# A ring of three for the modulation weights of the decode stage, and output weights ahead of the router's

## Chip, core and metric

One NeuronCore of a Trainium2 chip runs the whole step as one program. The metric is the device time of one execution in microseconds (us); the lower the better. PE is TensorE (PEld its weight loads), DVE VectorE, ACT ScalarE, POOL GpSimd, SP SyncE, which mostly issues DMAs.

## What is computed

One layer of a decoder step for a prompt of 2048 tokens and 8 decode tokens, in float32. What matters here is the decode side and the modulation:

```python
mod = (jax.nn.silu(c) @ w_ada + b_ada)[:, None, :]
sh1, sc1, gt1, sh2, sc2, gt2 = jnp.split(mod, 6, axis=-1)
...
s = jnp.einsum('bthe,btkhe->bthk', q, kg)     # decode: 8 tokens, three windows of 129 keys each
p = jnp.exp(s - m[..., None])
num = jnp.einsum('bthk,btkhe->bthe', p, vg)
...
conv = jax.nn.silu(layernorm(causal_dwconv(cext, conv_w, conv_b), ln_g, ln_b))
x = x + gt1 * (jnp.concatenate([att, conv], axis=-1) @ w_out)
h2 = rmsnorm(x, g_n2) * (1 + sc2) + sh2
x = x + gt2 * hierarchical_moe(h2, ...)
```

`w_ada` is 1024 x 6144 for 9 rows of `c` (8 decode rows and the prompt's). The first third, `sh1` and `sc1`, is made in the first stage; the other two thirds (gates and the second norm's vectors) are made in the decode stage.

## The kernel before

Stages follow one another, each in a block of its own with a barrier at its end: projection of all rows, attention of the prompt, the decode stage (`decode_mixers`), output projection and routing (`output_projection_and_routing`), experts, last norm. In a block every engine runs its own list of instructions in the order written, and semaphores tie them together.

**Decode stage** (L1187 to L1430). Keys, values and queries of the decode tokens (`dec_k`, `dec_v`, `dec_q`) were loaded during the attention stage.

- Modulation (L1384 to L1396): 16.8 MB of `w_ada` stream through `WAD`, a ring of two halves. A chunk is 512 of the 4096 columns; a half of it (512 of the 1024 rows, 1 MB, one DMA at L1253) is used by 16 matmuls `MPD<-WAD,CT` (four row blocks by four column quarters; the trace shows each as two, so x32 for a half); after both halves four matmuls add the bias `BAD` (L1395), ACT copies the sum from PSUM to `MOD_` (L1282), and after chunk 7 it is stored as `mod_rows` (L1298). SP issues a half when PE has used the one that was in its buffer (`w_used`).
- Scores (L1271, L1303 to L1327): for each of 8 batch entries b the product `dec_k` * `dec_q` (128x1536) and a sum over 64. POOL makes the products of odd b in `TMPP`, DVE those of even b in `TMP`, and DVE all the sums. Between them DVE makes the newest token's score: product QK, sum `S0D`, product `S0X` (two inputs in SBUF), which PE's first matmul (L1399) waits for.
- Convolution: DVE multiplies `ST` by the taps `CWR` (L1327), PE sums over the taps (L1408, `CP<-ST`).
- PE's order: N0 (L1399), chunks 0 to 3, transposed scores (L1404, `STP`), taps (L1408), transposed probabilities (L1412, `PTP`), L1415, chunks 4 and 5, values (L1422, `OD<-dec_v`), gathering (L1426), chunks 6 and 7.

**Output stage** (from L1433): for 17 tiles of rows a round mixes the three attention branches (`NB`, `STAT`) and the convolution's columns (`CC`), multiplies by `WO` (4 MB), normalises, and routes with `WR`. SP loads ahead of the rounds: 11 vectors (`GATE`, `GAIN`, `SHIFT` from `mod_rows`, `G2`, `LNG`, `LNB`, `BR`; L1507 to L1514), the first tile (L1519 to L1521), `WR`, `WO`, `lower`. DVE and POOL begin when all 11 vectors are in (`mods_in`); the load of the second tile waits until the first is mixed; PE's `project` (L1837) of the first tile stands behind `turn_conv` (L1818) of the second.

Of the kernel before, what the change touches and what calls it, by code (L numbers as in the profile page):

```python
# [13 lines left out]
AX = mybir.AxisListType  # L14
# [3 lines left out]
P = 128  # L18
SEQ = 2048
DEC = 8  # L20
D = 1024
KD = D // P
# [1164 lines left out]
def decode_mixers(nc, t, dr, const, const_at, state):  # L1187
# [7 lines left out]
    with ExitStack() as ctx:  # L1195
# [22 lines left out]
        WA, BA, MO = sb("WAD", [P, 2, KD // 2, 512]), sb("BAD", [1, 2, 512]), sb("MOD_", [P, NCH, P])  # L1218
        ada_in, b_in = ([sem(f"{x}{p}") for p in range(2)] for x in ("dec_ada_in", "dec_ada_b_in"))
# [16 lines left out]
        with nc.Block() as block:  # L1236
            @block.sync
            def _(sp):
                sp.dma_start(R[:], dr["dec"].rearrange("n b c -> b n c")).then_inc(rows_in, 16)
# [7 lines left out]
                w = t["w_ada"][0].rearrange("(k p) n -> p k n", p=P)  # L1247
# [12 lines left out]
                sp.dma_start(dr["mix"], MIX[:]).then_inc(mix_out, 16)  # L1260
                sp.wait_ge(mix_out, 16)
                sp.wait_ge(state_out, 32)

            @block.gpsimd
            def _(pool):
                pool.wait_ge(dq_in, 16)
                pool.wait_ge(dk_in, 48)
                for n, b in enumerate(range(1, DEC, 2)):
                    if n:
                        pool.wait_ge(odd_red, n)  # L1270
                    pool.tensor_tensor(TMPP[:], CK[:, b], QB[:, b, None, :].to_broadcast([P, 3, DATT]), ALU.mult).then_inc(odd_mul, 1)  # L1271
                pool.wait_ge(var_ready, 1)
                pool.tensor_tensor(VE[:], MV[:, 1:2], const("eps", DEC), ALU.add).then_inc(rs_ready, 1)
                pool.wait_ge(rs_ready, 1)
                pool.tensor_tensor(RS[:], VE[:], const("neghalf", DEC), ALU.pow).then_inc(rs_ready, 1)

            @block.scalar
            def _(act):
                def take_modulation(chunks):
                    for n in chunks:  # L1280
                        act.wait_ge(mod_in_psum, n + 1)
                        nc.scalar.copy(MO[:, n], MP[n % 2][:]).then_inc(mod_ready, 1)  # L1282

# [4 lines left out]
                nc.scalar.activation(PE_[:], SS[:], ACT.Exp, bias=NMD[:], scale=1.0, accum_out=LD[:]).then_inc(exp_ready, 1)  # L1288
                act.wait_ge(p8_psum, 1)
                nc.scalar.copy(P8[:], P8P).then_inc(p8_ready, 1)  # L1290
                take_modulation(range(4, 6))
                act.wait_ge(cstep, 7)
                nc.scalar.activation(TH[:], CVN[:], ACT.Tanh, scale=0.5).then_inc(th_ready, 1)
                take_modulation(range(6, NCH))
                act.wait_ge(mod_ready, NCH)
                for q in range(4):
                    out = dr["mod"][:, MOD_FIRST * 512:].rearrange("r (n q c) -> q r n c", q=4, c=P)
                    act.dma_start(out[q], MO[q * 32:q * 32 + DEC + 1]).then_inc(mod_out, 16)  # L1298
                act.wait_ge(mod_out, 64)

            @block.vector
            def _(dve):
# [6 lines left out]
                for n in range(DEC // 2):  # L1309
                    if n:  # L1310
                        dve.wait_ge(even_red, n)
                    nc.vector.tensor_tensor(TMP[:], CK[:, 2 * n], QB[:, 2 * n, None, :].to_broadcast([P, 3, DATT]), ALU.mult).then_inc(even_mul, 1)
                    dve.wait_ge(even_mul, n + 1)
                    reduced(2 * n, TMP, even_red)
                    if n == 0:
                        dve.wait_ge(rows_in, 16)
                        nc.vector.tensor_tensor(QK0[:], R[:, 0], R[:, 1], ALU.mult).then_inc(new_step, 1)
                        dve.wait_ge(new_step, 1)
                        nc.vector.tensor_reduce(S0[:], QK0[:].rearrange("b (h e) -> b h e", e=DH), AX.X, ALU.add).then_inc(new_step, 1)
                        dve.wait_ge(new_step, 2)  # L1320
                        nc.vector.tensor_tensor(S0X[:], const("samebatch", DEC).rearrange("b (a h) -> b a h", h=HEADS), S0[:, None, :].to_broadcast([DEC, DEC, HEADS]),
                                                ALU.mult).then_inc(new_spread, 1)
                    dve.wait_ge(odd_mul, n + 1)
                    reduced(2 * n + 1, TMPP, odd_red)
# [56 lines left out]
            def _(pe):  # L1381
                def modulation(chunks):
                    for n in chunks:
                        if n > 1:  # L1384
                            pe.wait_ge(mod_ready, n - 1)
                        for half in range(2):
                            pe.wait_ge(ada_in[half], n * 16 + 16)
                            for k in range(KD // 2):
                                for q in range(4):
                                    mm = nc.tensor.matmul(MP[n % 2][q * 32:q * 32 + 32], CT[:, half * KD // 2 + k], WA[:, half, k, q * P:q * P + P],  # L1390
# [9 lines left out]
                modulation(range(4))  # L1400
                pe.wait_ge(even_red, DEC // 2)
                pe.wait_ge(odd_red, DEC // 2)
                for n in range(3):
                    mm = nc.tensor.transpose(STP[:, n], SC[:, n], const("ident"))  # L1404
                mm.then_inc(s_turned, 1)
# [3 lines left out]
                mm.then_inc(conv_sum, 1)  # L1409
                pe.wait_ge(p_ready, 1)  # L1410
# [5 lines left out]
                modulation(range(4, 6))  # L1416
# [14 lines left out]
def output_projection_and_routing(nc, t, dr, const, const_at, state):  # L1431
# [27 lines left out]
    with ExitStack() as ctx:  # L1459
# [44 lines left out]
        with nc.Block() as block:  # L1504
            @block.sync
            def _(sp):
                for n, (dst, part) in enumerate(((GATE, 2), (GAIN, 4), (SHIFT, 3))):  # L1507
                    sp.dma_start(dst[:, 0], dr["mod"][DEC:DEC + 1, part * D:(part + 1) * D].to_broadcast([P, D])).then_inc(mods_in, 16)
                    sp.dma_start(dst[0:DEC, 1], dr["mod"][0:DEC, part * D:(part + 1) * D]).then_inc(mods_in, 16)
                sp.dma_start(G2[:], t["g_norm2"].to_broadcast([P, D])).then_inc(mods_in, 16)  # L1510
                sp.dma_start(LNG[:], t["ln_g"].to_broadcast([P, DCONV])).then_inc(mods_in, 16)
                sp.dma_start(LNB[:], t["ln_b"].to_broadcast([P, DCONV])).then_inc(mods_in, 16)
                sp.dma_start(BR[:, 0:GROUPS], t["b_router_group"].to_broadcast([P, GROUPS])).then_inc(mods_in, 16)
                sp.dma_start(BR[:, GROUPS:], t["b_router_expert"].to_broadcast([P, NEXP])).then_inc(mods_in, 16)  # L1514

# [106 lines left out]
            def _(act):  # L1622
# [21 lines left out]
                def route_exps(i):  # L1644
# [3 lines left out]
                    nc.scalar.activation(EV[:], DV[:], ACT.Exp).then_inc(gap_exp, 1)  # L1648

# [709 lines left out]
```

## Time and profile before

| what | value |
|---|---|
| median of 3 runs | 2475.18 us (2471.99 to 2478.70) |
| profiled execution, its own time | 2476.43 us |
| its span, first to last instruction | 2474.9 us |
| mean granted TensorE clock | 0.926 |
| decode stage, first DMA to first DMA of the next stage | 957.98 to 1037.33 us |
| of it PE busy, DVE busy, ACT busy, POOL busy (958 to 1037) | 41.73, 36.97, 3.66, 18.82 us |
| same stretch: DMA engines' busy share, rate | 0.71, 237 GB/s |
| output stage, first DMA to the first projection | 1037.33 to 1071.64 us |

The span is the sum of the stages, since barriers part them; so a stage is read by what its own last instruction waited for, not by the busy shares of the whole. A row of the timeline gives start, duration, engine, line, operation, what is written and read, and in brackets how long the engine had been idle and what ended that.

### The profile page before, as it was taken

Reading aid. Unit: us, or ns where it says so; the run is one execution under the profiler, and the core shown is the slowest. Engines: PE = TensorE matmul, PEld = TensorE weight load, DVE = VectorE, ACT = ScalarE, POOL = GpSimd, SP = SyncE. Lnnn points to the kernel's source line nnn. Section 1 sums busy time; section 2 is a strip of 40 time slices with the busy share of each in tenths; the row PEclk is TensorE's granted clock in tenths of the full one; section 3 lists DMA queues with packets and bytes.
Section 4 is the critical chain, followed back from the end, with each engine's and each line's share of the span. In section 5 each row is a group of like instructions: output and inputs, shape, how many; then the busy total and the mean of one; then the engine's idle time right before and its main releaser. Section 6 shows DMA issues by size and latency. Waiting matters only on the chain. (4 is left out here: it accounts for less than half of the span.)

```text
span 2474.9 us, 36684 instructions
## 1 busy us (share of the span) xinstructions
PE 2129.0 (86%) x11790; PEld 1630.7 (66%) x11791; DVE 1646.7 (67%) x3121; ACT 1099.2 (44%) x1979; POOL 642.1 (26%) x519
## 2 busy tenths in 40 slices
PE   5999999996999984459999939999999999999920
PEld 3788888885777773225555537888888888888810
DVE  2568888885666676147888656846563846656868
ACT  2311111114777781002222226856554757567833
POOL 1024444420111113035666521000000000000056
PEclk8999999998999996679999959999999999999965
DMA  8855555565664454668433156977765859658977
GB/s 267 276 193 187 187 187 203 192 207 193 203 235 135 140 181 163 227 257 312 131 130 128 70 196 246 398 263 263 262 234 190 315 214 353 251 208 300 397 271 297
DMA packets 220147, 560.78 MB, mean 227 GB/s; under 512 B 26685, under 2 KB 40341, under 8 KB 218904
## 3 DMA queue, kind: packets, MB, share of 16 engines
q1 hardware_dynamic: 179708, 439.45, 50.4%
q0 software_dynamic: 26016, 79.49, 8.9%
q10 hardware_dynamic: 14340, 40.78, 4.4%
q8 instruction: 46, 0.75, 0.1%
q14 instruction: 37, 0.30, 0.0%
HBM read 461.18 MB, written 171.04 MB: 255 GB/s over the span
## 5 line engine op out<-in xcount | busy, mean ns | idle before, releaser
L591 DVE SCALAR_TENSOR_TENSOR ARENA<-ARENA,TAPW 128x512 f32<-128x512 f32 (+3 forms) x493 | 293.3, 673 | 0.0
L1837 PE MATMUL OP<-WO,MT 128*128 128x512 f32 x544 | 258.3, 636 | 0.0
L417 POOL TENSOR_TENSOR MS<-SSQ,K 128x1 f32<-128x1 f32 x17 | 168.3, 9901 | 293.8 <-ACT H L460 293.8
L2103 DVE TENSOR_TENSOR GE<-SE,BE 128x256 f32<-128x256 f32 x98 | 36.8, 417 | 272.4 <-PE BE L2145 270.1
L1837 PEld LDWEIGHTS OP<-WO,MT 128*128 128x128 f32 x544 | 111.1, 208 | 135.7 <-issue 135.7
L710 PE MATMUL PJ<-WIN_H,HTH 128*128 128x512 f32 x680 | 174.0, 399 | 15.2 <-ACT HTH L466 11.7
L1017 ACT ACTIVATE PR<-SBX,NM 128x256 f32<-128x256 f32 (+1 forms) x384 | 171.9, 456 | 1.4 <-DVE NM L955 1.4
L2001 POOL DMA_INDIRECT XG<-h_rows,IDX x50 | 52.3, 1046 | 453.6 <-PE XP L2134 437.5
L714 PE MATMUL PJ<-WIN_H,HTL 128*128 128x512 f32 x680 | 168.4, 390 | 0.0
L718 PE MATMUL PJ<-WIN_L,HTH 128*128 128x512 f32 x680 | 168.0, 389 | 0.0
L492 ACT ACTIVATE ARENA<-PJ 128x512 f32<-128x512 f32 x51 | 30.4, 598 | 289.4 <-PE PJ L718 289.4
L710 PEld LDWEIGHTS PJ<-WIN_H,HTH 128*128 128x128 f32 x680 | 128.2, 191 | 46.6 <-ACT HTH L466 15.9
L2092 DVE TENSOR_TENSOR LO<-W1E,HI 128x2048 fp32r<-128x2048 f32 x64 | 143.6, 2283 | 3.9 <-ACT HI L2046 3.9
L714 PEld LDWEIGHTS PJ<-WIN_H,HTL 128*128 128x128 f32 x680 | 128.2, 189 | 27.0
L718 PEld LDWEIGHTS PJ<-WIN_L,HTH 128*128 128x128 f32 x680 | 127.6, 188 | 26.5
L2092 DVE TENSOR_TENSOR LO<-W3E,HI 128x2048 fp32r<-128x2048 f32 x64 | 143.6, 2284 | 0.6 <-ACT HI L2046 0.6
L2092 DVE TENSOR_TENSOR LO<-W2E,HI 128x2048 fp32r<-128x2048 f32 x64 | 143.6, 2284 | 0.0
L2046 ACT CAST HI<-W1E 128x2048 fp32r<-128x2048 f32 x64 | 120.1, 1902 | 31.1 <-DMA W1E<-in_w_expert_gate 30.6
L952 DVE CUSTOM_DVE_ANT_0 SBX<-S,BIAS 128x256 f32<-128x256 f32 (+1 forms) x384 | 117.4, 362 | 22.7 <-issue 22.7
L2046 ACT CAST HI<-W2E 128x2048 fp32r<-128x2048 f32 x64 | 120.6, 1912 | 25.2 <-ACT YE L2066 14.4
L2046 ACT CAST HI<-W3E 128x2048 fp32r<-128x2048 f32 x64 | 120.0, 1917 | 1.6 <-DMA W3E<-in_w_expert_up 1.5
L2013 POOL DMA_DIRECT2D IDX<-slot_tokens x48 | 27.4, 571 | 358.0 <-issue 247.2
(297 smaller groups left out, 4584.8 us busy)
## 6 DMA issues: line engine op xcount, KB each, us to landing
W1E<-in_w_expert_gate SPq DMA_DIRECT2D x64, 1024.0 KB
W3E<-in_w_expert_up SPq DMA_DIRECT2D x64, 1024.0 KB
W2E<-in_w_expert_down SPq DMA_DIRECT2D x64, 1024.0 KB, 11.3
expert_rows<-YE ACTq DMA_DIRECT2D x49, 512.0 KB, 5.7
expert_rows<-NOROWS POOLq DMA_DIRECT2D x3, 5632.0 KB, 20.8
WAD<-in_w_ada SPq DMA_DIRECT2D x16, 1024.0 KB, 5.4
X<-in_x_prompt SPq DMA_DIRECT2D x31, 512.0 KB
QN<-q_rows SPq DMA_DIRECT2D x48, 256.0 KB, 3.0
```

The lines of the kernel that those rows point to most:

```text
L417: pool.tensor_tensor(MS[:], SSQ[:], const("eps"), ALU.add).then_inc(ms_ready, 1)
L591: ins = nc.vector.scalar_tensor_tensor(out=out, in0=src, scalar=tap, in1=out, op0=ALU.mult, op1=ALU.add)
L710: nc.tensor.matmul(PJ[:, n], HTH[:, k], WH[:, n, k], start=k == 0, stop=False)
L714: nc.tensor.matmul(PJ[:, n], HTL[:, k], WH[:, n, k], start=False, stop=False)
L718: mm = nc.tensor.matmul(PJ[:, n], HTH[:, k], WL[:, n, k], start=False, stop=k == KD - 1)
L952: nc.vector.tensor_tensor_reduce(SBX[hh][:, h, 0:wide], SP_[hh][:, at_bank(h), 0:wide], bias, 1.0, -3e38, ALU.add, ALU.max, ml[:, head:hea ...
L1017: ins = nc.scalar.activation(PR[hh][:, h, 0:w], SBX[hh][:, h, 0:w], ACT.Exp, bias=NM[:, head:head + 1], scale=1.0, accum_out=ML[g.q][:, HE ...
L1837: mm = nc.tensor.matmul(OP[:, n * 512:(n + 1) * 512], MT[:, k], WO[:, k, n * 512:(n + 1) * 512], start=k == 0, stop=k == KD - 1)
L2001: pool.indirect_dma_start(XG[:], None, dr["h2"], bass.IndirectOffsetOnAxis(ap=IDX[:].bitcast(U32), axis=0)).then_inc(x_in, 16)
L2046: nc.scalar.copy(HI[n][:, cols], raw[n][:, cols]).then_inc(hi_ready[n], 1)
L2092: nc.vector.tensor_tensor(LO[n][:, cols], raw[n][:, cols], HI[n][:, cols], ALU.subtract).then_inc(lo_ready[n], 1)
L2103: nc.vector.tensor_tensor(G[:, cols], S[:, cols], BP[:, cols], ALU.mult).then_inc(g_ready, 1)
```

## The change

In the decode stage: the ring of `w_ada` has three buffers, each with its own semaphore, and half x is issued when half x-3 has been used; SP issues `DROWS`, then three halves, two biases, and only then the loads for the convolution, `OWN` last; the other six biases are issued by ACT behind its copies. POOL makes the products of b = 1, 3, 5, DVE the other five. DVE's order is written anew. PE's order: N0, chunks 0 and 1, taps, chunks 2 and 3, transposed scores, chunk 4, transposed probabilities, L1415's product, chunk 5, values, gathering, chunks 6 and 7. In the output stage the 11 vectors are issued by ACT instead of SP, and SP issues `WO` ahead of `WR`.

```diff
-        WA, BA, MO = sb("WAD", [P, 2, KD // 2, 512]), sb("BAD", [1, 2, 512]), sb("MOD_", [P, NCH, P])
-        ada_in, b_in = ([sem(f"{x}{p}") for p in range(2)] for x in ("dec_ada_in", "dec_ada_b_in"))
+        RINGS = 3
+        WA, BA, MO = sb("WAD", [P, RINGS, KD // 2, 512]), sb("BAD", [1, 2, 512]), sb("MOD_", [P, NCH, P])
+        ada_in, b_in = [sem(f"dec_ada_in{p}") for p in range(RINGS)], [sem(f"dec_ada_b_in{p}") for p in range(2)]
+        BY_POOL = (1, 3, 5)
...
             def _(sp):
+                def weights(x):
+                    n, half = divmod(x, 2)
+                    col = (MOD_FIRST + n) * 512
+                    if x >= RINGS:
+                        sp.wait_ge(w_used, x + 1 - RINGS)
+                    sp.dma_start(WA[:, x % RINGS], w[:, half * KD // 2:(half + 1) * KD // 2, col:col + 512]).then_inc(ada_in[x % RINGS], 16)
+
                 sp.dma_start(R[:], dr["dec"].rearrange("n b c -> b n c")).then_inc(rows_in, 16)
-                at, width = const_at["ownhead"]
-                sp.dma_start(OWN[:], t["constants"][:, at:at + width]).then_inc(own_in, 16)
+                for x in range(RINGS):
+                    weights(x)
+                for n in range(2):
+                    sp.dma_start(BA[:, n], t["b_ada"][0:1, (MOD_FIRST + n) * 512:(MOD_FIRST + n + 1) * 512]).then_inc(b_in[n], 16)
...
-                for n in range(NCH):
-                    col = (MOD_FIRST + n) * 512
-                    for half in range(2):
-                        if n:
-                            sp.wait_ge(w_used, n * 2 + half - 1)
-                        sp.dma_start(WA[:, half], w[:, half * KD // 2:(half + 1) * KD // 2, col:col + 512]).then_inc(ada_in[half], 16)
-                    if n > 1:
-                        sp.wait_ge(mod_in_psum, n - 1)
-                    sp.dma_start(BA[:, n % 2], t["b_ada"][0:1, col:col + 512]).then_inc(b_in[n % 2], 16)
+                at, width = const_at["ownhead"]
+                sp.dma_start(OWN[:], t["constants"][:, at:at + width]).then_inc(own_in, 16)
+                for x in range(RINGS, 2 * NCH):
+                    weights(x)
...
-                for n, b in enumerate(range(1, DEC, 2)):
+                for n, b in enumerate(BY_POOL):
...
                         nc.scalar.copy(MO[:, n], MP[n % 2][:]).then_inc(mod_ready, 1)
+                        if n + 2 < NCH:
+                            col = (MOD_FIRST + n + 2) * 512
+                            act.dma_start(BA[:, n % 2], t["b_ada"][0:1, col:col + 512]).then_inc(b_in[n % 2], 16)
...
+                own_scores(0)
+                dve.wait_ge(rows_in, 16)
+                nc.vector.tensor_tensor(QK0[:], R[:, 0], R[:, 1], ALU.mult).then_inc(new_step, 1)
+                pool_scores(0)
+                dve.wait_ge(new_step, 1)
...
+                own_scores(1)
                 dve.wait_ge(conv_in, 16 * 9)
                 nc.vector.tensor_tensor(ST[:], ST[:], CWR[:, None, :].to_broadcast([4 * TS, 2, DCONV]), ALU.mult).then_inc(taps_ready, 1)
+                pool_scores(1)
+                own_scores(2)
+                own_scores(3)
+                pool_scores(2)
+                own_scores(4)
...
             def _(sp):
-                for n, (dst, part) in enumerate(((GATE, 2), (GAIN, 4), (SHIFT, 3))):
-                    sp.dma_start(dst[:, 0], dr["mod"][DEC:DEC + 1, part * D:(part + 1) * D].to_broadcast([P, D])).then_inc(mods_in, 16)
...
                 load(0, 0)
+                sp.dma_start(WO[:], t["w_out"][0].rearrange("(k p) n -> p k n", p=P)).then_inc(weights_in, 16)
                 sp.dma_start(WR[:, :, 0:GROUPS], t["w_router_group"][0].rearrange("(k p) n -> p k n", p=P)).then_inc(weights_in, 16)
                 sp.dma_start(WR[:, :, GROUPS:], t["w_router_expert"][0].rearrange("(k p) n -> p k n", p=P)).then_inc(weights_in, 16)
-                sp.dma_start(WO[:], t["w_out"][0].rearrange("(k p) n -> p k n", p=P)).then_inc(weights_in, 16)
...
+                for n, (dst, part) in enumerate(((GATE, 2), (GAIN, 4), (SHIFT, 3))):
+                    act.dma_start(dst[:, 0], dr["mod"][DEC:DEC + 1, part * D:(part + 1) * D].to_broadcast([P, D])).then_inc(mods_in, 16)
```

TensorE in the decode stage, before, from chunk 3 to chunk 4 (a row `MPD<-WAD,CT` x32 is a whole chunk here, `MPD<-BAD,K` its bias):

```order
L1390 MATMUL MPD<-WAD,CT 32x128 x32
L1395 MATMUL MPD<-BAD,K 32x128 x4
L1404 MATMUL STP<-K,SC 64x128 x3
L1408 MATMUL CP<-ST,K 8x512 x2
L1412 MATMUL PTP<-K,SS 128x64 x3
L1415 MATMUL SMALLD<-P0X,K 8x8
L1390 MATMUL MPD<-WAD,CT 32x128 x32
```

and now, from the taps to chunk 5:

```order
L1427 MATMUL CP<-ST,K 8x512 x2
L1414 MATMUL MPD<-WAD,CT 32x128 x32
L1419 MATMUL MPD<-BAD,K 32x128 x4
L1414 MATMUL MPD<-WAD,CT 32x128 x32
L1419 MATMUL MPD<-BAD,K 32x128 x4
L1433 MATMUL STP<-K,SC 64x128 x3
L1414 MATMUL MPD<-WAD,CT 32x128 x32
L1419 MATMUL MPD<-BAD,K 32x128 x4
L1438 MATMUL PTP<-K,SS 128x64 x3
L1441 MATMUL SMALLD<-P0X,K 8x8
L1414 MATMUL MPD<-WAD,CT 32x128 x32
```

The taps' two matmuls (`CP<-ST`) moved ahead of chunks 2 and 3, and chunk 4 now stands between the transposed scores (`STP`) and the transposed probabilities (`PTP`).

VectorE at the start of the decode stage, before (the first product to the second POOL sum):

```order
L1312 TENSOR_TENSOR TMP<-dec_k,dec_q 128x1536
L1307 TENSOR_REDUCE SC<-TMP 128x3x8
L1317 TENSOR_TENSOR QK<-DROWS 8x512
L1319 TENSOR_REDUCE S0D<-QK 8x8
L1321 TENSOR_TENSOR S0X<-K,S0D 8x64
L1307 TENSOR_REDUCE SC<-TMPP 128x3x8
L1312 TENSOR_TENSOR TMP<-dec_k,dec_q 128x1536
```

and now:

```order
L1326 TENSOR_TENSOR TMP<-dec_k,dec_q 128x1536
L1319 TENSOR_REDUCE SC<-TMP 128x3x8
L1336 TENSOR_TENSOR QK<-DROWS 8x512
L1319 TENSOR_REDUCE SC<-TMPP 128x3x8
L1339 TENSOR_REDUCE S0D<-QK 8x8
L1341 TENSOR_TENSOR S0X<-K,S0D 8x64
L1326 TENSOR_TENSOR TMP<-dec_k,dec_q 128x1536
L1319 TENSOR_REDUCE SC<-TMP 128x3x8
L1345 TENSOR_TENSOR ST<-ST,CWR 120x1024
L1319 TENSOR_REDUCE SC<-TMPP 128x3x8
```

The sum of POOL's first product (`SC<-TMPP`) now stands ahead of `S0D` and `S0X`, and the taps' product (`ST<-ST,CWR`) in front of its second sum.

## Rows read from the trace of the kernel before

**Rows 1.** Stretch of the decode stage: us, busy PE, PEld, DVE, ACT, POOL; PEclk, DMA share, GB/s

```profile
969.90:997.40 27.50, 16.91 (x288) 11.61 (x288) 15.00 (x10) 0.80 (x3) 12.94 (x3) 0.56 0.86 290
```

**Rows 2.** Waits, 957.9 to 1031.6 us: total, times, longest

```profile
ACT MOD_ L1282 <- PE MPD L1395: 57.5, 8, 9.0
PE MPD L1390 <- DMA WAD<-in_w_ada: 23.2, 12, 4.2
```

**Rows 3.** Issue to landing, DMAs of L1253 (WAD), then of L1519 (NB)

```profile
DMA to landing us min/median/max: 5.0/5.4/8.7
...
DMA to landing us min/median/max: 4.3/4.6/11.8
```

**Rows 4.** Timeline, the modulation on SP's queue and PE

```profile
978.58 3.59 SPq L1253 DMA_DIRECT2D WAD<-in_w_ada  x2
983.80 1.93 PE L1390 MATMUL MPD<-WAD,CT 128*32 128x128 f32 x32 [1.48 <-DMA WAD<-in_w_ada]
991.09 1.94 PE L1390 MATMUL MPD<-WAD,CT 128*32 128x128 f32 x32 [0.94 <-DMA WAD<-in_w_ada]
1008.48 1.94 PE L1390 MATMUL MPD<-WAD,CT 128*32 128x128 f32 x32 [4.00 <-DMA WAD<-in_w_ada]
1011.17 1.42 PE L1390 MATMUL MPD<-WAD,CT 128*32 128x128 f32 x32 [0.75 <-DMA WAD<-in_w_ada]
1030.82 0.65 PE L1395 MATMUL MPD<-BAD,K 1*32 1x128 f32 x8
```

**Rows 5.** Timeline, products and scores on DVE and POOL

```profile
958.08 3.41 POOL L1271 TENSOR_TENSOR TMPP<-dec_k,dec_q 128x1536 f32<-128x1536 f32 x1 [10.90 <-POOLq L191]
958.10 5.00 DVE L1312 TENSOR_TENSOR TMP<-dec_k,dec_q 128x1536 f32<-128x1536 f32 x1 [13.60 <-PEq L191]
...
966.22 0.21 DVE L1321 TENSOR_TENSOR S0X<-K,S0D 8x64 f32<-8x64 f32 x1
...
968.02 1.74 DVE L1312 TENSOR_TENSOR TMP<-dec_k,dec_q 128x1536 f32<-128x1536 f32 x1
968.17 4.90 POOL L1271 TENSOR_TENSOR TMPP<-dec_k,dec_q 128x1536 f32<-128x1536 f32 x1 [6.68 <-DVE SC L1307]
...
988.27 1.22 DVE L1327 TENSOR_TENSOR ST<-ST,CWR 120x1024 f32<-120x1024 f32 x1
```

**Rows 6.** Timeline, PE's other work in the decode stage

```profile
997.43 0.85 PE L1404 MATMUL STP<-K,SC 128*64 128x128 f32 x3
998.21 3.58 PE L1408 MATMUL CP<-ST,K 120*8 120x512 f32 x4
1001.72 0.40 PE L1412 MATMUL PTP<-K,SS 64*128 64x64 f32 x3
1012.86 5.36 PE L1422 MATMUL OD<-dec_v,PTD 128*32 128x512 f32 x48
1019.14 0.42 PE L1390 MATMUL MPD<-WAD,CT 128*32 128x128 f32 x6
```

**Rows 7.** Timeline, SP's queue: first weights, first load of the next stage

```profile
963.36 0.95 SPq L1253 DMA_DIRECT2D WAD<-in_w_ada  x2
...
1037.33 0.36 SPq L1508 DMA_DIRECT2D GATE<-mod_rows  x1
```

**Rows 8.** Timeline, start of the output stage

```profile
1046.96 5.17 SPq L1550 DMA_DIRECT2D WR<-in_w_router_expert  x1
1050.76 2.35 DVE L1673 SCALAR_TENSOR_TENSOR GAIN<-GAIN,G 128x1024 f32<-128x1024 f32 x2 [29.92 <-DMA BR<-in_b_router_expert]
1052.18 0.95 SPq L1551 DMA_DIRECT2D WO<-in_w_out  x1
...
1064.03 0.49 SPq L1521 DMA_DIRECT2D CC<-conv_cols  x1
...
1070.73 1.12 PE L1818 MATMUL CP<-K,CC 128*128 128x128 f32 x4 [5.10 <-DMA CC<-conv_cols]
```

**Rows 9.** Stretch of the output stage, columns as in Rows 1

```profile
1048.00:1053.00 5.00, 0.00 (x0) 0.00 (x0) 2.24 (x2) 0.00 (x0) 0.00 (x0) 0.50 0.77 213
```

More of the change, by code:

```diff
@@ L1238, in _ @@
             def _(sp):
+                w = t["w_ada"][0].rearrange("(k p) n -> p k n", p=P)
+                def weights(x):
[4 more added lines that the diff above has]
+                    sp.dma_start(WA[:, x % RINGS], w[:, half * KD // 2:(half + 1) * KD // 2, col:col + 512]).then_inc(ada_in[x % RINGS], 16)
                 sp.dma_start(R[:], dr["dec"].rearrange("n b c -> b n c")).then_inc(rows_in, 16)
-                at, width = const_at["ownhead"]
-                sp.dma_start(OWN[:], t["constants"][:, at:at + width]).then_inc(own_in, 16)
+                for x in range(RINGS):
+                    weights(x)
+                for n in range(2):
+                    sp.dma_start(BA[:, n], t["b_ada"][0:1, (MOD_FIRST + n) * 512:(MOD_FIRST + n + 1) * 512]).then_inc(b_in[n], 16)
                 for b in range(4):
@@ L1288, in _ @@
                 nc.scalar.activation(PE_[:], SS[:], ACT.Exp, bias=NMD[:], scale=1.0, accum_out=LD[:]).then_inc(exp_ready, 1)
+                take_modulation(range(4, 5))
                 act.wait_ge(p8_psum, 1)
                 nc.scalar.copy(P8[:], P8P).then_inc(p8_ready, 1)
-                take_modulation(range(4, 6))
+                take_modulation(range(5, 6))
                 act.wait_ge(cstep, 7)
@@ L1307, in reduced, with own_scores @@
                     nc.vector.tensor_reduce(SC[:, :, b * HEADS:(b + 1) * HEADS], tmp[:].rearrange("p n (h e) -> p n h e", e=DH), AX.X, ALU.add).then_inc(done, 1)
-                for n in range(DEC // 2):
+                own = [b for b in range(DEC) if b not in BY_POOL]
+                def own_scores(n):
                     if n:
                         dve.wait_ge(even_red, n)
-                    nc.vector.tensor_tensor(TMP[:], CK[:, 2 * n], QB[:, 2 * n, None, :].to_broadcast([P, 3, DATT]), ALU.mult).then_inc(even_mul, 1)
+                    nc.vector.tensor_tensor(TMP[:], CK[:, own[n]], QB[:, own[n], None, :].to_broadcast([P, 3, DATT]), ALU.mult).then_inc(even_mul, 1)
@@ L1313, in _ @@
                     dve.wait_ge(even_mul, n + 1)
[L1314 to L1322, printed above, removed]
@@ L1323, in _, with pool_scores @@
-                    dve.wait_ge(odd_mul, n + 1)
-                    reduced(2 * n + 1, TMPP, odd_red)
+                    reduced(own[n], TMP, even_red)
+                def pool_scores(n):
+                    dve.wait_ge(odd_mul, n + 1)
+                    reduced(BY_POOL[n], TMPP, odd_red)
+                own_scores(0)
+                dve.wait_ge(rows_in, 16)
+                nc.vector.tensor_tensor(QK0[:], R[:, 0], R[:, 1], ALU.mult).then_inc(new_step, 1)
+                pool_scores(0)
@@ L1326, in _ @@
+                dve.wait_ge(new_step, 1)
+                nc.vector.tensor_reduce(S0[:], QK0[:].rearrange("b (h e) -> b h e", e=DH), AX.X, ALU.add).then_inc(new_step, 1)
+                dve.wait_ge(new_step, 2)
+                nc.vector.tensor_tensor(S0X[:], const("samebatch", DEC).rearrange("b (a h) -> b a h", h=HEADS), S0[:, None, :].to_broadcast([DEC, DEC, HEADS]),
+                                        ALU.mult).then_inc(new_spread, 1)
+                own_scores(1)
                 dve.wait_ge(conv_in, 16 * 9)
@@ L1386, in modulation @@
                         for half in range(2):
-                            pe.wait_ge(ada_in[half], n * 16 + 16)
+                            x = 2 * n + half
+                            pe.wait_ge(ada_in[x % RINGS], x // RINGS * 16 + 16)
                             for k in range(KD // 2):
                                 for q in range(4):
-                                    mm = nc.tensor.matmul(MP[n % 2][q * 32:q * 32 + 32], CT[:, half * KD // 2 + k], WA[:, half, k, q * P:q * P + P],
+                                    mm = nc.tensor.matmul(MP[n % 2][q * 32:q * 32 + 32], CT[:, half * KD // 2 + k], WA[:, x % RINGS, k, q * P:q * P + P],
                                                           start=half == 0 and k == 0, stop=False)
@@ L1399, in _ @@
                 nc.tensor.matmul(N0P, S0X[:].rearrange("b a h -> b (a h)"), const("ones", DEC)[:, 0:1], start=True, stop=True).then_inc(new_psum, 1)
[L1400 to L1405, printed above, removed]
+                modulation(range(2))
                 pe.wait_ge(taps_ready, 1)
@@ L1409, in _ @@
                 mm.then_inc(conv_sum, 1)
+                modulation(range(2, 4))
+                pe.wait_ge(even_red, DEC - len(BY_POOL))
+                pe.wait_ge(odd_red, len(BY_POOL))
+                for n in range(3):
+                    mm = nc.tensor.transpose(STP[:, n], SC[:, n], const("ident"))
+                mm.then_inc(s_turned, 1)
+                modulation(range(4, 5))
                 pe.wait_ge(p_ready, 1)
@@ L1415, in _ @@
                 nc.tensor.matmul(P8P, const("ofbatch", BH), P0X[:], start=True, stop=True).then_inc(p8_psum, 1)
-                modulation(range(4, 6))
+                modulation(range(5, 6))
                 pe.wait_ge(ptd_ready, 1)
@@ L1506, in _ @@
             def _(sp):
-                for n, (dst, part) in enumerate(((GATE, 2), (GAIN, 4), (SHIFT, 3))):
-                    sp.dma_start(dst[:, 0], dr["mod"][DEC:DEC + 1, part * D:(part + 1) * D].to_broadcast([P, D])).then_inc(mods_in, 16)
[L1509 to L1514, printed above, removed]
                 def load(i, row):
@@ L1648, in route_exps @@
                     nc.scalar.activation(EV[:], DV[:], ACT.Exp).then_inc(gap_exp, 1)
+                for n, (dst, part) in enumerate(((GATE, 2), (GAIN, 4), (SHIFT, 3))):
+                    act.dma_start(dst[:, 0], dr["mod"][DEC:DEC + 1, part * D:(part + 1) * D].to_broadcast([P, D])).then_inc(mods_in, 16)
+                    act.dma_start(dst[0:DEC, 1], dr["mod"][0:DEC, part * D:(part + 1) * D]).then_inc(mods_in, 16)
+                act.dma_start(G2[:], t["g_norm2"].to_broadcast([P, D])).then_inc(mods_in, 16)
+                act.dma_start(LNG[:], t["ln_g"].to_broadcast([P, DCONV])).then_inc(mods_in, 16)
+                act.dma_start(LNB[:], t["ln_b"].to_broadcast([P, DCONV])).then_inc(mods_in, 16)
+                act.dma_start(BR[:, 0:GROUPS], t["b_router_group"].to_broadcast([P, GROUPS])).then_inc(mods_in, 16)
+                act.dma_start(BR[:, GROUPS:], t["b_router_expert"].to_broadcast([P, NEXP])).then_inc(mods_in, 16)
                 act.sem_inc(x2_out, 16)
```

1 line of the change is left out of this document (removed).

## The prediction

> **What bounds the kernel now.** The stages are separated by barriers, so what a stage saves comes off the span. I read first the busy time of the engines in stretches, then the waits of the decode stage, then its timeline, then the same for the start of the output stage. From 969.9 to 997.4 us PE was busy 16.91 of 27.5 us, its granted clock mostly the lower of the two, while the DMA engines were 0.86 busy at 290 GB/s [rows 1]. PE's own waits name the cause: 23.2 us for the weights WAD; ACT waited 57.5 us for the finished sums, so it has room [rows 2]. The stage is a queue of 16 halves of 1 MB (8 chunks of two), numbered 0 to 15 here. A half takes 5.4 us (median) from issue to landing [rows 3], 5.2 where nothing is ahead of it (half 4, issued at 978.58, used from 983.80); PE uses it in 1.93 us [rows 4].
>
> With two buffers a buffer comes round in 5.2 + 1.93, about 7.2 us: half 4 starts at 983.80, half 6 at 991.09, 7.29 apart, so 3.6 us for each half [rows 4]. Yet two halves that are both in the queue land 2.69 us apart (1008.48 and 1011.17) [rows 4]. So the depth of the ring, not the transfer, sets the pace. Besides, the ring stands still when TensorE turns to other work: half 12 lands late behind one such pause, halves 14 and 15 behind another.
>
> **The ring of three.** Three halves per 7.2 us would be 2.4 us each; the transfer needs 2.6 to 2.7. I take 2.6, a bound by transfer. The first half is issued at about 958.4, where it was 963.36 (DROWS goes ahead of it at 958.0) [rows 7]; halves 0, 1, 2 land near 963.6, 966.2, 968.8. This early start is mostly lost, though, since PE's first matmul waits for S0X:
>
> **DVE and POOL.** Where POOL's product of 128x1536 started first (958.08, 3.41 us), DVE's took 5.00 us and ended 1.6 us after it; where DVE's started first (968.02, 1.74 us), POOL's took 4.90 [rows 5]. The two products with both inputs in SBUF exclude each other. Now DVE adds up POOL's first product before it makes S0 and S0X; so POOL's second product starts at about 967.4, while DVE is in the 0.67 us sum S0, and S0X, a product of two SBUF tiles, waits for its end at 970.8. S0X ends at 971.0 instead of 966.4 [rows 5]. The trace shows no small product behind a POOL product; if S0X is not held, it ends at 968.2, and the whole timetable is 2.7 earlier. I take 971.0, by the nearest row, the held product of 5.00.
>
> Scores: DVE now makes 5 products and 8 sums of 1.75, 1.55 for the new token and 1.22 for the taps (25.5), plus 3.3 held at the start, 2.6 at S0X, 1.6 at its fourth product: from 958.1 to about 991.2, against 988.3 before (the taps started at 988.27) [rows 5]. PE asks for them only after chunk 3, so 3 us later costs nothing while chunk 3 ends after 991.2. The loads for the taps now stand behind 3 MB of weights, 0.8 MB that should be in by 972; DVE asks for them at 974.6.
>
> **Timetable of PE** (landing = the later of issue + 5.2 and the half before + 2.6; a bias 0.65 [rows 4]). Halves 0 to 2 run from 971.4 to 977.8 with the bias of chunk 0. Half 3, issued at 973.4, lands at 978.6; chunk 1 ends at 981.2. Then the taps' matmuls, moved here: 3.6 us [rows 6], to 984.8; they are not hidden, since half 4 is there at 981.2. Halves 4, 5, 6 follow to 991.2; half 7 (issued 986.8) lands at 992.0; chunk 3 ends at 994.6. Transposing the scores takes 0.85 [rows 6]. Chunk 4 (halves 8, 9, both there) fills 995.4 to 999.9; DVE's softmax meanwhile needs 3.4 from the end of the transposes (998.3 to 1001.7 before [rows 6]), done at 998.8, so this wait of PE goes. Turning the probabilities takes 0.6. Chunk 5 (half 11, issued 997.4, lands at 1002.6) ends at 1005.1. The values and their gathering take 6.3 (1012.86 to 1019.14 [rows 6]): 1011.4. Halves 12 to 14 were fetched meanwhile. Half 15 can be issued only when 12 is used, at 1013.4, and lands at 1018.6; chunk 7 ends at 1021.1. Before, it ended at 1031.5 (1030.82 + 0.65 [rows 4]). **Term 1: -10.4 us.** The way from there to the next stage (its first load at 1037.33 [rows 7]) is unchanged: 5.9. The two copies of the convolution state and the store of MIXD follow half 15 on SP, at about 1014 to 1016, covered by halves 14 and 15 and those 5.9 us.
>
> Six biases of 2 KB move to ACT, 0.4 us each behind a copy: ACT has 57.5 us of waits, and each bias has two chunks of time. Nothing. If a bias landed late, PE would wait with two halves in hand. OWN goes last and is asked for at 1010: nothing.
>
> **The output stage.** ACT now issues the 11 loads of vectors (2.73 MB, 5.7 us of issuing, while it has nothing to do), SP starts with the branch rows at once and issues the 4 MB WO before WR. Before, WR's second issue held SP from 1046.96 for 5.17 us, WO was issued at 1052.18, and from 1048 to 1053 the DMA engines moved only 213 GB/s [rows 8, 9]; that hole is now filled. DVE starts with GAIN when all 11 are in, at 1050.76 [rows 8]. They now share the engines with the rows and WO. If they are held back only by their own gaps, they land as before; if the queues share evenly, 5.5 MB must move at some 400 GB/s (1.05 MB in 2.6 us), 13.7 us, with 2.6 around it (what a half's 5.2 has beyond its transfer): 1053.6, +2.9. I take +1.5, the middle, since both ends rest on one stretch each. On the other side, the second tile's columns were issued at 1064.03 behind WO and landed at 1070.7, 6.7 us, and PE's first projection follows at once [rows 8]. With WO gone from the queue I take 4.7 (the rows NB before them land in 4.6 as a median [rows 3]): -2.0. **Term 2: -0.5 us**, bounds -3.3 and +2.9.
>
> A page speaks against this term. By the Trainium skill, "DMA: Bandwidth & Descriptors" (queues, rings and completion order), each DMA engine takes packets in turn from the queues that have work, and issuing from more engines saves issue time only. By this rule alone the vectors come 2.9 later and term 2 is +0.9; the low 213 GB/s of [rows 9] says that there was idle time to fill, which the rule leaves open.
>
> **Sum:** -10.9. The profiled execution (span 2474.9, its own time 2476.43) would become 2465.5; it lay 1.25 above the median of 2475.18, so the predicted median is 2464.3. About 0.3%, 7.4 us, can be told from no change.
>
> **Rivals.**
> A. S0X is not held: 2.7 better, term 1 is -13.1: 2461.6. For it: no row shows a small product held. Against: the product of 5.00. Chance 0.10.
> B. Transfer rate: with three in flight a half still needs 3.6 us, as from 969.9 to 997.4. Then half 11 lands at 978.6 + 8 x 3.6 = 1007.4, half 15 at 1021.8, end 1024.3: term 1 is -7.2, 2467.5. For it: the DMA share of 0.86 [rows 1]. Against: halves 2.69 apart [rows 4]. Chance 0.15.
> C. The loads for the taps come late behind the weights, and DVE, waiting in order, holds all later scores. It decides from 978 on (3.4 us of slack before chunk 3's end); at 981 the scores come at 997.6, 3 us late: 2467.3. Chance 0.10.
> D. Slower: the vectors of the output stage starve behind WO, WR and the rows and land when all is in, at about 1066 (WO then took to 1052.18 + 13), 15.3 us later than 1050.76, and POOL and DVE wait for them. With term 1 that is +4.9: 2480. It makes the kernel slower once the delay is over 10.4, and by more than 0.3% from 17.8. For it: one queue of 4 KB rows against many small ones. Against: the vectors are issued at the same time as the rows. Chance 0.07.
> My forecast has 0.58, its own bounds from 2460 to 2468.
>
> **Chances.** Faster by over 0.3% (below 2467.8): 0.9 of the forecast, all of A, a third of B, half of C: 0.72. Slower by over 0.3%: half of D, 0.03. Within: 0.25. The range 2460.0 to 2472.0 holds the forecast, A, B and C and leaves out D and mishaps of more than 8 us.
>
> **What would show it.** Right: halves of WAD about 2.6 us apart in PE's timeline; S0X ending near 971; its first weights waiting for PE, not PE for them; the score transposes right behind chunk 3 at 994 to 995; PE's wait before turning the probabilities gone; the output stage's first load near 1027; GAIN 13.5 to 16.5 after it (13.4 before); PE's first projection 34 after it. Wrong: a wait of DVE for the loads of the taps, or of PE for a bias; halves 3.6 apart; GAIN more than 17 us after the start; SP held by WR's issue beyond the moment the second tile's rows are wanted.

## The result, and the profile after

The change makes the kernel faster: 2462.79 us (median of 12 runs, 2458.63 to 2470.12) against 2476.94 us before (12 runs), ratio 0.9947 with the 95% interval 0.9936 to 0.9958, so 14.1 us; repeated later, 0.9944 (0.9930 to 0.9957). The forecast was 10.9 us.

| stage, from its first DMA to the next stage's | before | after | difference |
|---|---|---|---|
| the two stages ahead of the decode stage | 957.98 | 955.79 | -2.19 |
| decode | 79.35 | 67.38 | -11.97 |
| output projection and routing | 412.08 | 411.96 | -0.12 |
| experts | 919.54 | 920.08 | +0.54 |
| last norm | 105.95 | 105.19 | -0.76 |
| span | 2474.9 | 2460.4 | -14.5 |

The change touches only the second and third of these. The first row shows how far one execution of the same code can differ from another: over the 14 profiles of this case the decode stage starts 952.29 to 958.92 us after the start of the span, though none of them changes what comes ahead of it. The decode stage in stretches (columns as in [rows 1]), then its waits:

```profile
969.90:997.40 27.50, 19.72 (x358) 12.83 (x350) 21.77 (x21) 2.04 (x7) 4.88 (x1) 0.75 0.99 337
```

```profile
ACT MOD_ L1290 <- PE MPD L1419: 43.4, 8, 8.3
...
PE MPD L1414 <- DMA WAD<-in_w_ada: 11.1, 8, 3.0
```

Against [rows 1] the DMA engines went from 0.86 to 0.99 busy and from 290 to 337 GB/s; PE's waits for weights fell from 23.2 to 11.1 us. The timeline of DVE, POOL and PE in the decode stage after the change:

```profile
965.03 3.42 POOL L1279 TENSOR_TENSOR TMPP<-dec_k,dec_q 128x1536 f32<-128x1536 f32 x1 [5.73 <-DVE SC L1319]
965.58 2.94 DVE L1341 TENSOR_TENSOR S0X<-K,S0D 8x64 f32<-8x64 f32 x1
...
972.36 1.22 DVE L1345 TENSOR_TENSOR ST<-ST,CWR 120x1024 f32<-120x1024 f32 x1 [0.38 <-DMA LBD<-in_ln_b]
...
977.62 1.88 PE L1427 MATMUL CP<-ST,K 120*8 120x512 f32 x4
...
986.45 1.94 PE L1414 MATMUL MPD<-WAD,CT 128*32 128x128 f32 x32 [0.67 <-DMA WAD<-in_w_ada]
986.96 1.75 DVE L1319 TENSOR_REDUCE SC<-TMP 128x24 f32<-128x1536 f32 x1
...
989.05 1.94 PE L1414 MATMUL MPD<-WAD,CT 128*32 128x128 f32 x32 [0.66 <-DMA WAD<-in_w_ada]
...
991.26 0.52 PE L1433 MATMUL STP<-K,SC 128*64 128x128 f32 x3
...
1001.85 5.36 PE L1448 MATMUL OD<-dec_v,PTD 128*32 128x512 f32 x48
...
1015.18 1.94 PE L1414 MATMUL MPD<-WAD,CT 128*32 128x128 f32 x32 [3.02 <-DMA WAD<-in_w_ada]
1017.05 0.65 PE L1419 MATMUL MPD<-BAD,K 1*32 1x128 f32 x8
```

Halves 6 and 7 come 2.60 us apart, where halves came 3.6 apart ([rows 4]: 983.80 and 991.09 for two of them). That is the best pair, though: half 4 was used at 980.18, so halves 4 to 7 come 2.96 us apart on average. S0X, 0.21 us in [rows 5], lasted 2.94: POOL's product had started 0.55 us before S0X did, and S0X ended 0.07 us after the product. DVE's last sum of scores ends at 988.71, and PE turns to the scores (`STP`) only at 991.26. The last half is waited for, as forecast, but for 3.02 us, where the timetable has 0.7 (half 14 used up at 1017.9, half 15 there at 1018.6): PE was through half 14 in 1.08 us instead of 1.93, at the higher clock. The start of the output stage:

```profile
1023.17 0.37 SPq L1536 DMA_DIRECT2D NB<-branch_rows  x1
...
1025.43 7.81 SPq L1567 DMA_DIRECT2D WR<-in_w_router_group  x1
...
1033.28 11.32 SPq L1568 DMA_DIRECT2D WR<-in_w_router_expert  x1
...
1041.65 2.35 DVE L1699 SCALAR_TENSOR_TENSOR GAIN<-GAIN,G 128x1024 f32<-128x1024 f32 x2 [31.82 <-DMA BR<-in_b_router_expert]
...
1053.47 0.48 SPq L1538 DMA_DIRECT2D CC<-conv_cols  x1
...
1058.69 1.12 PE L1844 MATMUL CP<-K,CC 128*128 128x128 f32 x4 [3.64 <-DMA CC<-conv_cols]
```

GAIN starts 18.48 us after the stage's first DMA (13.43 in [rows 7, 8]), 5.05 later; the second tile's columns land in 5.22 us instead of 6.7; PE's first projection comes at 36.43 instead of 34.31.

### The profile page after: what moved, and what is told of

Its sections match the earlier page's. It is cut to its first block and busy times, and to the rows that moved or that the text cites. A ratio compares the mean times of both kernels' runs of the same rounds, so it can differ in the third digit from the quotient of the medians.

```text
span 2460.4 us, 36684 instructions
## 1 busy us (share of the span) xinstructions
PE 2119.0 (86%) x11790; PEld 1625.5 (66%) x11791; DVE 1650.2 (67%) x3122; ACT 1098.9 (45%) x1979; POOL 634.2 (26%) x518
## 5 line engine op out<-in xcount | busy, mean ns | idle before, releaser
L710 PE MATMUL PJ<-WIN_H,HTH 128*128 128x512 f32 x680 | 173.9, 398 | 14.5 <-ACT HTH L466 11.7
L710 PEld LDWEIGHTS PJ<-WIN_H,HTH 128*128 128x128 f32 x680 | 128.1, 191 | 45.9 <-ACT HTH L466 15.9
```

The lines of the kernel that those rows point to most:

```text
L710: nc.tensor.matmul(PJ[:, n], HTH[:, k], WH[:, n, k], start=k == 0, stop=False)
```

## Experiments

All are measured against the kernel before; "stage" is the decode stage in the profiled execution, of which each run has one. Of the same code its length varies: 79.35 and 82.49 us for the old one (before, e2), 67.08 to 68.73 us in four of five executions of the new one (after, e1, e3, e11) and 72.40 in the fifth (e4). A difference of a few microseconds between two stages is therefore no proof by itself; where it is used below, the timeline inside the stage is shown for it.

### Which half of the change: e1_decode_only, e2_output_only

```diff
 e1: decode_mixers of the change, output_projection_and_routing of before
 e2: decode_mixers of before, output_projection_and_routing of the change
```

> The change's decode stage alone, output stage as before. Theory: the decode stage is 67.4 us long (first DMA to the next stage's first DMA) as in the full change, 12.0 shorter than the 79.35 of before, and the output stage keeps its 412.1 us with GAIN 13.4 us and the first projection 34.3 us after its start: 12 us faster than before, 0.995. Rival 1 (the output part of the change costs 2 us, as its first projection 2.1 later says): this kernel is 2 us faster than the full change. Rival 2 (the output part gains 2, as forecast with its lower bound): it is 2 us slower than the full change.

> The change's output stage alone, decode stage as before. Theory: decode stage 79.4 us; GAIN 18.5 us and the first projection 36.4 us after the output stage's start (13.4 and 34.3 before), the stage as a whole 411.9 as in the full change, since the next rounds wait for DMAs anyway: same time as before. Rival 1: 2 us slower, stage 414. Rival 2: 2 us faster.

e1: 2460.38 us, ratio 0.9929 (0.9915 to 0.9943); stage 67.08. e2: 2476.14 us, ratio 0.9994 (0.9985 to 1.0003); GAIN at 16.61 and the first projection at 34.18 us. So the whole gain is the decode stage's, and the output part is worth nothing that can be told on its own.

### What makes the output part: e3_wo_first, e4_vectors_act, e11_change_again

```diff
 e3 (on e1's output stage):
-                WR (two loads), WO
+                WO, WR (two loads)          # the 11 vectors stay on SP
 e4 (on the change):
-                WO, WR (two loads)
+                WR (two loads), WO          # the 11 vectors stay on ACT
 e11: the change itself
```

> New decode stage; output stage with WO ahead of WR but the 11 vectors on SP as before. If sharing the DMA engines between two queues made GAIN late (theory), GAIN is back at 13.4 us after the start, WO's early issue fills the hole, the second tile's columns land in about 5.2 instead of 6.7 us, and the first projection comes at about 32.8: 1.5 better than e1_decode_only. Rival (WO itself in front costs as much as it gives, since WR's small packets then run alone later): first projection at 34 or later.

> New decode stage; output stage with the 11 vectors on ACT but WR ahead of WO as before. Theory (WO's 4 MB take half of the engines from the vectors): WR's issue holds WO back by 6 us or more, so GAIN comes at 15 to 16 us after the start, between 13.4 and 18.5. Rival (two queues of small packets, WR and BR, hinder each other): GAIN stays at 18 or later.

> The change itself once more beside the others, for the output stage. Theory (its output part costs 1.5 to 2 us against that of before): GAIN at 16.6 to 18.5 and first projection at 34.2 to 36.4 us after the stage's start again, and the time 1 to 3 us above e1_decode_only's 2460.4. Rival (no cost): the time within 1 us of it. Decode stage 67 to 69 us.

| output stage | GAIN after start, us | first projection after start, us |
|---|---|---|
| as before (before, e1, e6, e7, e8) | 12.24 to 13.43 | 33.43 to 34.31 |
| of the change (after, e2, e5, e11) | 16.61 to 18.48 | 34.18 to 36.43 |
| vectors on SP, WO first (e3, e9, e10) | 11.61 to 13.92 | 32.22 to 34.57 |
| vectors on ACT, WR first (e4, e12) | 14.43, 14.64 | 32.33, 32.40 |

In time e3 is 2462.83 us (ratio 0.9931, 0.9914 to 0.9948) and e4 2459.54 (0.9924, 0.9909 to 0.9940); neither can be told from e1. The vectors are late by 3 to 5 us only where they go on ACT's queue and WO stands ahead of WR on SP's; with WR first, whose issue held SP for 7.84 us in e12, WO starts 10.1 us into the stage and the vectors are 1.0 to 1.2 us late. That supports the sharing of the DMA engines with WO. e3's gain of 1.5 did not come again in e9 and e10. In time, e11 (2462.43) and the change lie 2 us above e1, with overlapping intervals; the mean first projection of the four is 1.6 us later (35.4 against 33.8). So the output part costs one to two microseconds at the first tile. Little of it reaches the end of the stage: from its first load to the experts' first load the stage took 408.66 to 412.08 us in the five profiles with the output part of before (mean 410.6) and 411.03 to 412.09 in the four with that of the change (mean 411.6). The means are 1.0 apart, inside the spread of the same code.

### Ring or order: e5_ring_two, e6_ring_only, e8_old_pe_order

```diff
 e5 (on the change):
-        RINGS = 3
+        RINGS = 2
 e6 (on before; each buffer with a semaphore of its own, and PE's index to match):
-        WA = sb("WAD", [P, 2, KD // 2, 512])
+        WA = sb("WAD", [P, 3, KD // 2, 512])
+                        x = 2 * n + half
+                        if x > 2:
+                            sp.wait_ge(w_used, x - 2)
 e8 (on e1), PE, in short; ACT's copies follow the same order:
-                modulation(range(2)); taps; modulation(range(2, 4)); scores turned; modulation(range(4, 5)); probabilities turned; modulation(range(5, 6))
+                modulation(range(4)); scores turned; taps; probabilities turned; modulation(range(4, 6))
```

> The full change with a ring of two again. Theory (the ring carries most of the gain): a half every 3.6 us again; only the wait before the probabilities and the taps' matmuls are still covered, so the decode stage is 75 to 77 us, about 9 more than the 67.4 of the full change and 3 less than before. Rival (order of work carries it): 71 us or less.

> The kernel before with a ring of three and nothing else. Theory: halves 2.6 to 2.8 us apart up to chunk 3, which ends near 33 us after the stage's start (39.5 before); taps and softmax hold PE as before, the stage is 69 to 71 us. Rival (the early start and the order carry the gain): 75 or more.

> New decode stage but PE's order of before (taps after the scores, probabilities ahead of chunks 4 and 5); output stage as before. Theory: taps (1.9 to 3.6 us) and the softmax (3.4, partly beside the taps) are uncovered again, but the three buffers fill meanwhile and are used faster than they come, so the stage is only 1 to 3 us longer than 67.1. Rival (the order matters more than the ring): 4 us or more.

e5: 2476.69 us, ratio 0.9999 (0.9987 to 1.0011), stage 83.02. The rest of the change without the third buffer gains nothing that can be told; the 3 us expected for it did not appear. PE in e5, weights of chunks 1 and 2:

```profile
977.77 1.94 PE L1414 MATMUL MPD<-WAD,CT 128*32 128x128 f32 x32 [3.64 <-DMA WAD<-in_w_ada]
981.21 1.93 PE L1414 MATMUL MPD<-WAD,CT 128*32 128x128 f32 x32 [1.50 <-DMA WAD<-in_w_ada]
```

Its half 2 is used 20.3 us into the stage (19.2 before). It could be issued only when half 0 had been used, and PE could not begin before S0X, which POOL held until 12.74 us. So SP issued half 2 at 972.52, 15.1 us into the stage, and it was used 5.25 us later; the small loads were through by then, the DMA engines stood at 0.24 busy from 969.43 to 971.43 and idle for the 2 us after. By this timeline the early issue buys two halves only, and the hold of S0X costs what they gain. A ring of two without that hold was not run, so e5 shows that the rest of the change as it stands needs the third buffer, and not that no order of work could gain without it.

e6: 2464.96 us, ratio 0.9952 (0.9934 to 0.9969), stage 71.34: the third buffer alone gives 8.0 of the 12.0 in the stage, and in time it can't be told from the whole change (0.9947). Its chunk 3 ends 34.5 us into the stage, no later than that of the change (35.5; before 39.5), so up to there the third buffer gives all of it. By the end of chunk 5 it is 3.2 us behind the change, and the values, which ran partly at the low clock (6.75 against 5.36 us), add 1.4; what follows gives 0.6 back. In e6, PE's halves 2 and 3 are 2.70 us apart:

```profile
974.92 1.94 PE L1392 MATMUL MPD<-WAD,CT 128*32 128x128 f32 x32 [0.20 <-DMA WAD<-in_w_ada]
977.62 1.93 PE L1392 MATMUL MPD<-WAD,CT 128*32 128x128 f32 x32 [0.77 <-DMA WAD<-in_w_ada]
```

The mean from half 2 to half 7 is 2.89 us in e6, 3.57 in the kernel before.

e8: 2466.18 us, ratio 0.9949 (0.9933 to 0.9965), stage 72.42, 5.3 more than e1; the expected 1 to 3 fell. Its interval overlaps with e1's (0.9915 to 0.9943). Its PE:

```profile
994.29 0.85 PE L1427 MATMUL STP<-K,SC 128*64 128x128 f32 x3
995.06 3.57 PE L1431 MATMUL CP<-ST,K 120*8 120x512 f32 x4
998.57 0.40 PE L1435 MATMUL PTP<-K,SS 64*128 64x64 f32 x3
...
999.02 1.95 PE L1413 MATMUL MPD<-WAD,CT 128*32 128x128 f32 x64
...
1006.78 1.94 PE L1413 MATMUL MPD<-WAD,CT 128*32 128x128 f32 x32 [4.44 <-DMA WAD<-in_w_ada]
```

For the 4.7 us from 994.29 to 999.02 no buffer comes free. The three full ones are then used in a burst, and PE waits 4.44 us for half 11, whose issue had to wait for the first of the burst. (1.4 of the 5.3 are the values, which ran in part at the low clock, 6.78 against 5.36 us.) A pause of PE longer than the ring's stock is a pause of the transfer: that is what the new order removes. Since one stage length proves little, the stretch in question is compared over all profiles: from the end of chunk 3 to the end of chunk 5 PE took 14.75 us in e6 and 14.94 in e8, with three buffers and the old order, and 10.59 to 13.57 in the eight profiles with three buffers and the change's order (after, e1, e3, e4, e7, e9, e11, e12). So the order gives 1.2 to 4.4 us there. With two buffers and the change's order (e5) the stretch took 14.41, against 15.43 and 16.82 with the old.

### PE's start and the scores: e7_s0x_early, e9_taps_on_act, e10_chunk4_first

```diff
 e7 (on e1), DVE:
-                own_scores(0); QK; pool_scores(0); S0; S0X; own_scores(1)
+                own_scores(0); QK; S0; S0X; pool_scores(0); own_scores(1)
 e9 (on e7; WO first): the nine loads for the taps and OWN
-                sp.dma_start(...)
+                act.dma_start(...)          # ahead of ACT's first copy
 e10 (on e9), PE, in short; ACT's copies follow the same order:
-                modulation(range(2, 4)); scores turned; modulation(range(4, 5)); probabilities turned; modulation(range(5, 6))
+                modulation(range(2, 5)); scores turned; modulation(range(5, 6)); probabilities turned
```

> New decode stage with S0X made ahead of the sum of POOL's first product; output stage as before. Theory (S0X was held by POOL's product): S0X takes 0.2 instead of 2.94 us and ends 8.4 us after the stage's start instead of 12.7, PE's first weights are used at 9 instead of 13, chunk 3 ends 3 us earlier, and the stage is 64 us, 3 less than e1_decode_only's 67.1. Rival (the loads behind the first three halves and the scores set the pace, not PE's start): the stage stays within 1 us of 67.

> e7_s0x_early with the nine loads for the taps and OWN issued by ACT, so that nothing stands between half 2 and half 3 on SP's queue; output stage with WO first and the vectors on SP (as e3_wo_first). Theory (in e7 half 3 came 9 us after its buffer was free because the slow small loads stood ahead of it): half 3 is used from about 16.5 instead of 19.65 us, chunk 3 ends near 32 when the scores are ready, and the decode stage is 64 to 65 us, 3 less than 67.1 to 67.9. Rival (the small loads take the engines' time from whichever queue, by turns): half 3 comes at 19 as before and the stage stays at 67. Output stage: first projection at 32.2 again.

> e9_taps_on_act with chunk 4 ahead of the transposed scores and chunk 5 between scores and probabilities. Theory (with the weights early, DVE's scores at 32 us are the next bound and PE has a chunk to do meanwhile): 1 to 3 us less than e9_taps_on_act, about 62 us. Rival (the weights are the bound, the scores are not waited for): no difference within 1 us.

e7: 2460.57 us, ratio 0.9929 (0.9916 to 0.9943), stage 67.85. S0X ended at 8.45 us again and PE began 4.3 us earlier, as expected, but the stage did not shrink: the rival holds. SP's queue and PE in e7:

```profile
968.97 35.97 SPq L1249 DMA_DIRECT2D WAD<-in_w_ada  x12
```

```profile
977.82 1.94 PE L1414 MATMUL MPD<-WAD,CT 128*32 128x128 f32 x32 [5.87 <-DMA WAD<-in_w_ada]
```

Half 3 was issued at 968.97 and used at 977.82, 8.85 us later instead of 5.2: the loads for the taps stood ahead of it. From 968.17 to 974.17 the DMA engines were fully busy but moved only 235 to 257 GB/s, against 385 to 390 in the 2 us before and after. Half 3 came 19.65 us into the stage, in e1 20.31. DVE, too, waited 3.31 us for these loads, and its scores were done at 991.41, only 0.7 us before PE turned to them: in e7 rival C of the prediction is close to holding.

e9 (2462.79 us, 0.9944, 0.9930 to 0.9958; stage 66.25) took these loads to ACT's queue. Half 3 came at 19.35, not 16.5, because now halves 1 and 2 came late:

```profile
967.73 1.94 PE L1414 MATMUL MPD<-WAD,CT 128*32 128x128 f32 x32
972.85 1.94 PE L1414 MATMUL MPD<-WAD,CT 128*32 128x128 f32 x32 [3.18 <-DMA WAD<-in_w_ada]
```

Half 1 was used 13.93 us into the stage. The bytes ahead of half 3 take the engines' time from whichever queue. The stage is the shortest of all, but by less than the spread, and the time shows nothing. e10 (2459.76 us, 0.9941, 0.9926 to 0.9957; stage 67.98) has a stage 1.7 us longer than e9's instead of 1 to 3 shorter, and the times can't be told apart: the scores are not waited for. The change's own timeline says the same, with 2.55 us between the last sum (988.71) and the transposes (991.26).

### A candidate: e12_best

```diff
 e12: decode_mixers of e7, output stage of e4
```

> The candidate that should beat the change: decode stage of e7_s0x_early, output stage of e4_vectors_act (vectors on ACT, WR ahead of WO). Theory: decode stage 67 to 69 us (S0X early gives nothing, the weights' transfer is the bound), GAIN about 14.4 and first projection about 32.3 us after the output stage's start, as in e4_vectors_act, so about 3 us better than the change: 2459 to 2460. Rival (32.2 of e3_wo_first did not come again in e9_taps_on_act with 33.95, so 32.3 was chance too): first projection at 34, time 2460 to 2462, not to be told from e1_decode_only.

2461.56 us, ratio 0.9939 (0.9925 to 0.9952), stage 67.02, first projection at 32.40 as in e4. Its span, 2456.6 us, is 3.8 below the change's, but in time it can be told neither from e1 (0.9929) nor from the change. The kernel with all the gain that was shown and nothing more is e1: the decode stage of the change with the output stage of before.

## Why the prediction was right

- **Term 1** was -10.4, measured -11.97 (one profile against one; against e2's profile of the old stage it would be -15.1). The mechanism is as told: the third buffer quickens the ring (e6), the order covers the pauses (e6 and e8 against the rest). The pace was taken too fast, 2.6 us a half; single pairs came so, but the mean was 2.96 in the change (halves 4 to 7) and 2.89 in e6 (2 to 7), against 3.57 before. Against the timetable, all from the stage's start (forecast, then measured): chunk 1 ends at 23.2, 21.9; the taps at 26.8, 23.7; chunk 3 at 36.6, 35.5; chunk 5 at 47.1, 46.1; chunk 7 at 63.1, 61.9. The taps were mis-sized: 3.6 us taken from a row at the low clock, 1.88 measured. Of the 3.1 us that PE was then ahead of the timetable 2.0 were gone by the end of chunk 3: it waited 0.68 us for half 4 and 2.40 for half 5. That the end came out within 1.2 us is in part luck: a slower ring and matmuls at the higher clock (halves of 1.08 instead of 1.93 us) offset each other. The way to the next stage took 5.5 instead of 5.9.
- **S0X held by POOL**: right, forecast to end at 13.0 us, measured 12.73 (and 8.45 without the hold in e7). The step built on it, that the early start "is mostly lost" by it, and with it rival A's price of 2.7 us, was wrong: e7 removed the hold and gained nothing, since half 3 is late by the loads ahead of it (8.85 us from issue to use). The timetable let a half land by its issue and the half before alone and left out the small loads in between.
- **Scores** 3 us later cost nothing: right. They were done 32.9 us into the stage (forecast 33.2), 2.55 us before PE asked for them.
- **The biases on ACT, OWN last**: nothing, right; no wait for either in PE's or DVE's rows.
- **Term 2** was -0.5 with bounds -3.3 and +2.9; the first projection came 2.1 later. Within the bounds, but the step "I take +1.5" for the vectors was wrong: +5.05 in this profile and +3.2 to +5.1 in the four of its kind, beyond the mark of 17 us set as a sign of error in three of four. The page's rule of engines taking turns (the Trainium skill, "DMA: Bandwidth & Descriptors", queues, rings and completion order) gave +2.9 for the vectors and +0.9 for the term and was nearer; e4 and e12 agree with its direction, the vectors being 1.0 and 1.2 us late where WO was issued 10 us into the stage. What the forecast missed on the other side: the first tile's columns were turned before GAIN, so the mix was 1.45 us shorter (10.87 us from GAIN to the second tile's load against 12.32), and 1.5 came from the faster landing. That the shorter mix was there to offset the vectors is luck. Over the whole stage -0.12 is left, close to the -0.5, and by e2 (ratio 0.9994) nothing that can be told.
- **Rival B** (3.6 us a half) fell: the mean was 2.96, with the DMA engines 0.99 busy; the truth lies nearer to the forecast's 2.6 than to it. Its price was also added up wrongly: with half 11 landing at 1007.4, half 12 is used up at 1018.2, so that half 15, 5.2 us later, lands at 1023.4 and not 1021.8, the end is 1026.0, and B would have been about 2469, not 2467.5. **C** fell (a wait of 0.38 us for the loads of the taps, chunk 3 not held), **D** fell: the vectors were late by a third of what it asked.
- 2.2 of the profile's 14.5 us lie ahead of the changed stages and are chance. Of the measured 14.1, 12 are explained by the decode stage in these two profiles; the other 2 are within the interval (10.4 to 15.9), and the old stage measured 82.49 in its second profile.

What stays open: whether the output part costs anything in time; why the old decode stage took 82.49 us in e2 and 79.35 in the first profile (1.24 of the 3.1 us are the values, 6.60 against 5.36; the rest is not explained); what a ring of two gains when S0X is not held; whether a fourth buffer would help. The last two were not run.

## What to carry to other kernels

Work out a ring's depth from its round trip: depth times the transfer time of a piece must reach issue to landing plus use (here 7.2 us, which two pieces of 2.6 us miss and three reach). After that, look for pauses of the consumer longer than the ring's stock, and for other loads ahead of the ring's in any queue; the order of work that fills such pauses paid here with three buffers, and the same code with two gained nothing. When an early start is what you want, look for what holds the consumer's first step: in e5 the third half could not be issued before 15.1 us into the stage, because PE waited for S0X. A load that the first tile waits for came 3 to 5 us late when it shared the DMA engines with a large one that is needed later, so issue the large one behind it.

## What was not expected of the hardware

The same 48 matmuls of the values took 5.36 us in nine of the 14 profiles, before, after and e1 among them, and 6.58 to 7.14 us in e2, e4, e5, e6 and e8. In e4 the granted clock was 0.75 over the stretch with them, between its two levels (1.2 and 2.4 GHz), in e1 1.00:

```profile
1005.41 7.14 PE L1448 MATMUL OD<-dec_v,PTD 128*32 128x512 f32 x48
```

```profile
1005.00:1013.00 8.00, 8.00 (x58) 1.91 (x54) 1.07 (x3) 0.90 (x2) 0.00 (x0) 0.75 0.60 222
```

The code of the stage does not decide it: the old one gave 5.36 (before) and 6.60 us (e2), the change's 5.36 (after, e1) and 7.14 (e4). Nor does a steady supply of weights just ahead: in the kernel before, PE had waited 4.00 us for a half shortly before the values ([rows 4], 1008.48) and they still took 5.36. What decides it is not shown; it is worth up to 1.8 us in a stage's length and belongs in its error. And the issue of WR, a load of small rows in two parts, held SP for 7.8 and 11.3 us in the change, where WO stood ahead of it and the vectors ran beside it. Before, it held SP for 1.1 and 5.2 us; with WO ahead but the vectors on SP (e3) for 4.4 and 7.1, with the vectors beside it but WO behind (e12) for 0.7 and 7.8. So the issue took longest where both were there. It hurt nothing here because SP's next load was wanted later still: WR's issue ends at 1044.60, and the second tile's load is issued at 1052.52.
